# Moving the stage buffers to the bottom of SBUF and everything that lives throughout above them

## The reference

```python
def swiglu_ffn(h, w_gu, w_down):
    gate, up = jnp.split(h @ w_gu, 2, axis=-1)       # 1024 -> 2 x 2816
    return (jax.nn.silu(gate) * up) @ w_down         # 2816 -> 1024

for i in range(2):
    x = x + 0.5 * swiglu_ffn(rms_norm(x, norm_g[i, 0]), ffn_w_gu[i, 0], ffn_w_down[i, 0])
    h = rms_norm(x, norm_g[i, 1])
    x = x + (gla_mixer(h, ...) if i == 0 else diff_mixer(h, ...))
    x = x + 0.5 * swiglu_ffn(rms_norm(x, norm_g[i, 2]), ffn_w_gu[i, 1], ffn_w_down[i, 1])
...
x = x + gate * (concat([y_lru, y_att]) @ w_out)      # the hybrid layer
```

## Time and profile before

| | us |
|---|---|
| median of three runs | 2256.18 |
| the profiled execution, whole | 2258.16 |
| its span, first to last instruction | 2256.3 |
| TensorE (PE) busy | 2230.7 |
| VectorE (DVE) busy | 1260.9 |
| ScalarE (ACT) busy | 918.7 |
| GpSimd (POOL) busy | 155.6 |

### The profile page before, as it was taken

How to read it: one execution, slowest core, us unless ns; L and a number is a source line. 1 busy time by engine, 2 the same in 40 slices (tenths; PEclk the granted TensorE clock), 3 DMA queues, 4 the chain that set the end, 5 groups by cost and what they waited for, 6 DMA issues and landing times.

```text
span 2256.3 us, 24793 instructions
## 1 busy us (share of the span) xinstructions
PE 2230.7 (99%) x9880; PEld 1788.9 (79%) x9880; DVE 1260.9 (56%) x1958; ACT 918.7 (41%) x1446; POOL 155.6 (7%) x128
## 2 busy tenths in 40 slices
PE   9999999999999999999999999999999999999999
PEld 7888888877688888888888887777678888877777
DVE  6443445978654434454434446777566535555863
ACT  4322233567433223333322235777443223237672
POOL 3000003000030000030000021000120000020000
PEclk9999999999999999999999999999999999999999
DMA  6223224121135242242223223222134434232221
GB/s 207 87 84 112 98 70 133 38 94 57 43 101 177 66 133 82 70 136 93 76 94 112 84 84 110 73 73 91 56 122 152 137 112 131 89 131 70 63 73 38
DMA packets 201763, 217.40 MB, mean 96 GB/s; under 512 B 4984, under 2 KB 194552, under 8 KB 201648
## 3 DMA queue, kind: packets, MB, share of 16 engines
q1 hardware_dynamic: 194960, 193.48, 26.4%
q0 software_dynamic: 6544, 22.26, 2.9%
q10 hardware_dynamic: 144, 0.08, 0.0%
HBM read 213.66 MB, written 6.32 MB: 97 GB/s over the span
## 4 chain that ended last, share of the span: by engine, by line
PE 94%; DVE 3%; ACT 2%; issue 1%; DMA 0%; SPq 0%; DVEq 0%; ACTq 0%
PE ps L1606 92%; PE ps L1610 1%; ACT sb_xh L638 1%; DVE sb_xl L1095 0%; ACT sb_whi L638 0%; DMA sb_xT<-xT 0%; DVE sb_wlo L1090 0%; ACT sb_hyb_th L638 0%; ACT sb_lnb L638 0%; DVE sb_hyb_rq L1496 0%; DVE sb_hyb_q L1510 0%; ACT sb_hyb_pt L638 0%; ACT sb_hyb_k L638 0%; ACT sb_dif_k L638 0%; DVE sb_dif_p L1383 0%
## 5 line engine op out<-in xcount | busy, mean ns | idle before, releaser
L1606 PE MATMUL ps<-sb_xh,sb_whi 128*128 128x512 f32 x2120 | 844.9, 399 | 12.8 <-DVE sb_xl L1397 4.9
L1606 PE MATMUL ps<-sb_xl,sb_whi 128*128 128x512 f32 x2120 | 828.6, 391 | 0.1
L1606 PE MATMUL ps<-sb_xh,sb_wlo 128*128 128x512 f32 x2120 | 824.1, 391 | 0.0
L1090 DVE TENSOR_TENSOR sb_wlo<-sb_raw,sb_whi 128x1024 fp32r<-128x1024 f32 (+2 forms) x401 | 473.7, 1185 | 484.3 <-ACT sb_whi L638 483.1
L638 ACT ACTIVATE sb_whi<-sb_raw 128x1024 fp32r<-128x1024 f32 (+2 forms) x401 | 386.9, 968 | 568.5 <-PE ps L1606 561.5
L1606 PEld LDWEIGHTS ps<-sb_xh,sb_whi 128*128 128x128 f32 x2120 | 399.5, 188 | 105.3 <-issue 17.3
L1606 PEld LDWEIGHTS ps<-sb_xl,sb_whi 128*128 128x128 f32 x2120 | 399.8, 189 | 87.3 <-issue 4.6
L1606 PEld LDWEIGHTS ps<-sb_xh,sb_wlo 128*128 128x128 f32 x2120 | 399.3, 188 | 85.3
L1606 PE MATMUL ps<-sb_ffn_ah,sb_whi 128*128 128x512 f32 x704 | 277.6, 394 | 0.0
L1606 PE MATMUL ps<-sb_ffn_ah,sb_wlo 128*128 128x512 f32 x704 | 276.0, 392 | 0.0
L1606 PE MATMUL ps<-sb_ffn_al,sb_whi 128*128 128x512 f32 x704 | 273.3, 388 | 0.0
(11 more groups left out here) (259 smaller groups left out, 1769.2 us busy)
## 6 DMA issues: line engine op xcount, KB each, us to landing
sb_raw<-ffn_w_gu SPq DMA_DIRECT2D x86, 1024.0 KB, 5.2
sb_raw<-ffn_w_down SPq DMA_DIRECT2D x32, 1024.0 KB, 4.9
sb_raw<-gla_w_in SPq DMA_DIRECT2D x12, 1024.0 KB, 5.3
sb_raw<-diff_w_in SPq DMA_DIRECT2D x12, 1024.0 KB, 5.2
sb_ada_raw<-w_ada POOLq DMA_DIRECT2D x12, 1024.0 KB, 6.3
sb_raw<-w_in SPq DMA_DIRECT2D x10, 1024.0 KB, 5.3
sb_raw<-ffn_w_down SPq DMA_DIRECT2D x16, 512.0 KB, 3.6
sb_raw<-ffn_w_down SPq DMA_DIRECT2D x16, 256.0 KB, 2.7
```

The lines of the kernel that those rows point to most:

```text
L1090: e.tensor_tensor(lo, raw[panel % NRAW][:, 0:nk, off:off + 128], hi.bitcast(F32), ALU.subtract).then_inc(sem["w_lo"], 1)
L1606: return e.matmul(out, lhsT, rhs, start=start, stop=stop, skip_group_check=skip)
```

## The change

The list of tensors that stay open is moved below the stages' blocks in the code, and behind a placeholder `stages` of 21,792 float32 (87,168 bytes) per partition that covers the same bytes as the largest stage. The stages' common base becomes 16,512. Within the list the order changes as well: `xh`, `xl`, `xT`, the small tensors, the weight slots, and `raw` at the top. Two lists that name `sqs` and `sq` are completed after these are opened. The instructions of the built program and their order on each engine are the same; only addresses differ.

```diff
+STAGE = 21792
...
-        raw = [sb(f"raw{i}", [128, KT, 256]) for i in range(NRAW)]
-        whi = [sb(f"whi{i}", [128, KT, 128], F32R) for i in range(NSLOT)]
-        wlo = [sb(f"wlo{i}", [128, KT, 128], F32R) for i in range(NSLOT)]
-        x = sb("xT", [128, KT, S])
-        xh = sb("xh", [128, KT, S], F32R)
-        xl = sb("xl", [128, KT, S], F32R)
-        par = sb("par", [128, NCOLS])
...
-            hpb = [t_(f"p{i}", [128, S]) for i in range(2)] + [sqs]
+            hpb = [t_(f"p{i}", [128, S]) for i in range(2)]
...
+        sb("stages", [128, STAGE])
+        xh = sb("xh", [128, KT, S], F32R)
+        xl = sb("xl", [128, KT, S], F32R)
+        x = sb("xT", [128, KT, S])
+        par = sb("par", [128, NCOLS])
+        cst = sb("cst", [128, 3, 128])
+        rb = sb("rb", [128, S])
...
+        whi = [sb(f"whi{i}", [128, KT, 128], F32R) for i in range(NSLOT)]
+        wlo = [sb(f"wlo{i}", [128, KT, 128], F32R) for i in range(NSLOT)]
+        raw = [sb(f"raw{i}", [128, KT, 256]) for i in range(NRAW)]
+        hpb.append(sqs)
```

More of the change, by code:

```diff
@@ L478, in build @@
             lw = HPT[:, 0:2, :].rearrange("p j (t c) -> p j t c", c=128)
-            lru_ln = [HPT[:, 2, :], HPT[:, 3, :], sq[:, :], HPT[:, 0, :]]
             hst = [t_(f"st{i}", [128, 8]) for i in range(3)]
+        sb("stages", [128, STAGE])
[5 more added lines that the diff above has]
+        rb = sb("rb", [128, S])
+        lnb = sb("lnb", [128, S])
+        sqs = sb("sqs", [128, S])
+        sq = sb("sq", [128, S])
+        small = sb("small", [128, 96])
+        ada = sb("ada", [128, 24])
+        lam, neg_b, rbcol = small[:, 56:64], small[:, 64:72], small[:, 72:76]
+        ones, ident, blk = cst[:, 0, :], cst[:, 1, :], cst[:, 2, :]
+        bias_vec = nc.dram_tensor("bias_vec", (8, 1024), F32).ap()
+        bias_rep = nc.dram_tensor("bias_rep", (8, 128 * 1024), F32).ap()
+        whi = [sb(f"whi{i}", [128, KT, 128], F32R) for i in range(NSLOT)]
+        wlo = [sb(f"wlo{i}", [128, KT, 128], F32R) for i in range(NSLOT)]
+        raw = [sb(f"raw{i}", [128, KT, 256]) for i in range(NRAW)]
+        hpb.append(sqs)
+        lru_ln = [HPT[:, 2, :], HPT[:, 3, :], sq[:, :], HPT[:, 0, :]]
         first_squares = rb[:, :], lnb[:, :], ffn_mem[0][3][1][:, :]
```

## The result

The changed kernel takes 2291.47 us (median of 4, 2289.76 to 2294.18) against 2256.27 us before (2255.85 to 2256.99): a ratio of 1.0157, 95% interval 1.0139 to 1.0174. It is slower by 35 us where I forecast 6 us faster, and far outside the range. The profiled execution took 2292.99 us, its span 2291.2 us, 34.9 us more than before.

What follows compares the result with a forecast made beforehand. TensorE bounds the kernel; 5.6 + 0.5 + 0.3 = 6.4 us gained, less a little for reappearing waits, 6.2 us, takes the median from 2256.18 to 2250.0 us. Forecast's own range 2248.3 to 2251.7, overall 2247.5 to 2263.

Steps and rivals of the forecast that it cites:

- What bounds the kernel: Whole kernel: TensorE is busy 2230.7 of 2256.3 us; only the time per matmul and 25.6 us of waits can move.
- Stage tiles as moving operands: Down projections and hybrid's output projection: 2304 matmuls each lose a 2.6 ns price for beginning at 64 modulo 128; 5.6 us gained.
- the passages: Switches between x and stage tiles, eight each way: their extra time goes if all tiles cost the same; 0.5 us gained.
- Weights at 64 modulo 128: Weight slots' new remainder under all 8664 matmuls: taken to cost nothing, from the interval 1397.86 to 1398.09, 230 against 226.6 ns.
- The upper bound: Most the weights' new remainder could cost: the moving operand's 2.6 ns for each of 8664 matmuls, 22.5 us.
- only the offset between moving tile and weights counts: Case inside a slower rival (2272.5 us, chance 0.09): offset 64 in the slow stretches before, 64 in all after.
- the weights' place: Rival, slower: weights' new address costs what the moving operand's does, 16.3 us more, 2272.5 us; chance 0.09.
- 64 everywhere: Claim within a slower rival: after the change, every moving tile lies at offset 64 from its weights.
- The border at byte 131,072: Rival, slower: tiles above that byte are slow, so upper `xl` tiles become slow; 2252.1 to 2267.5 us; chance 0.14.
- No part: Rival, no change: addresses don't matter, down projections are slower by something that goes with the stage; 2256.2 us; chance 0.10.
- Scores: Mixers' `dif_k`, `dif_kl` matmuls (0.4 us) with linear attention's plain float32 matmuls and transposes (0.2 us): half counted, 0.3 us gained.
- VectorE, DMA: Weights' split and panel loads at new addresses: hidden under 10.9 us of TensorE per panel, cost nothing; mixers' waits +-0.5 us.

## Why the prediction was wrong

*What bounds the kernel.* Right: the chain is PE's, and the 34.9 us of the span match the 35.1 us by which the records of the x matmuls grew. The observation on which I built was right too: 226.6 ns in one kind of stretch and 229.2 in the other, the same in every window, is an effect of addresses and not of contention: 192 bytes of padding took it away.

*Stage tiles as moving operands.* This step failed. I gave the 2.6 ns to the moving tile's own remainder modulo 128. The stages' tiles got remainder 0 and kept 229 ns; with everything moved by 64 bytes it stayed so. What held was the distance to the weights: 64 before, 64 modulo 256 after. With 192 bytes of padding it becomes 0, and then the gain that I worked out for this step (5.6 us, and 0.5 for the passages) is there: 2250.5 us against the forecast 2250.0. The size was right, and the cause wrong; that the gain came to the forecast's number in that layout says nothing for the remainder.

*Weights at 64 modulo 128.* This is the failed step that made the loss: a term that I took as nothing and that measured 35 us. I took nothing, on one interval of the earlier trace rows in which `dif_q` is loaded while `xh` streams; the distance is 192 there, and matmuls alone, with all weights at that distance, take 233.4 ns. The row reads 230 at two decimals and I called it no cost. One interval can't show it. In the trace it is 226 ns, and the four of the scores behind it are 228, 230, 233 and 231: what the switch cost came after the interval that I read. In the same way, single intervals of a steady down projection are 232, 226 and 229 ns in turn, and only their mean, 229, is the price. The upper bound was wrong as well. It took the 2.6 ns of distance 64 for the worst that an address can do, and the other distances cost 6 to 8 ns. At 7 ns, 8664 matmuls are 61 us and not 22.5. The loss of 6360 x 5.5 ns = 35 us lies between, since only the x tiles came to such a distance. What the runs showed in the place of this step: not where the weights lie, but that they no longer lie at distance 0 from x. That distance went to 192 modulo 256, at which an x matmul takes 233.5 ns instead of 226.6.

*The rivals.* I named the mechanism, "only the offset between moving tile and weights counts", with 0.09 in one rival with the weights' place, and wrote "64 everywhere" after the change. That was read modulo 128. Modulo 256 the two were 192 and 64, and I had both tables of addresses. The price followed from the wrong modulus. "64 everywhere" would have made x as slow as the stages, 229 ns; it became 233.5. The border at byte 131,072 is excluded twice: the stages' tiles, now below it, stayed slow, and with all at 0 the upper tiles of `xl` and the weights lie above it and are fast. "No part" is excluded by the 192 bytes, with which every tile still begins on a 16-byte line. By the Trainium skill (TensorE: Matmul & The Clock Gate, on what happens when you issue a matmul) the two read ports keep a weight load from slowing the stream; here the distance alone makes 226.6 or 234.3 ns with nothing else running, so the measurement decides, at least for float32r.

*Scores, passages, VectorE, DMA.* The scores of `dif_k` with `dif_q` kept their time (455 and 456 ns); both operands moved together, so their distance stayed, and the 0.3 us that I took for them had the same wrong cause. The passages lost their extra price, as I had taken it, though x and the stages still differ in their distance: in the changed kernel the first twelve intervals after a switch to stage tiles take 2.75 us, which is 12 x 229 ns, and those after the way back 2.79, no more than 12 x 233.5; in the kernel before they were 2.76 and 2.77, of which 2.72 would be 12 x 226.6. That is half a microsecond beside the 35. That the weights' split and the DMA stay hidden was right.

*What remains open.* What in TensorE is slowed, and which operands' distance it is. Neither the distance to a matmul's own weights, nor that to the weights loaded meanwhile, nor each change of remainder explains all settings. In the steady settings short and long intervals follow in a fixed order (232, 226, 229 ns at distance 64), which suggests that something carries over from one matmul to the next; what, no run here shows. Shown are the period of 256 bytes, that 0 is the fast distance at 512 columns, and that the same distance costs the same, within 1 ns, in every layout tried.

## What to carry to other kernels

Before trusting a layout, list for each hot matmul the start of the moving tile minus the start of the weights, modulo 256. In float32r with 512 columns keep it at 0; a change that "only moves buffers" can cost 1.6%, and 192 bytes of padding can give 0.25%. At 256 columns 0 was not the fast distance, so other shapes need their own measurement. When a trace shows two levels of one operation, write down every relation of its addresses, own remainders and differences, at several moduli, before naming one the cause; and do not bound an unknown by the one price that happens to be visible.

## What was not expected of the hardware

A float32r matmul of 512 columns with its own LDWEIGHTS takes 226.6 ns from start to start at best and 228.9 to 234.3 ns at other distances; a start 4 bytes off is already out of the fast place (232.6 ns). The same in bfloat16 takes 216 ns at any distance tried. That is the gap which the Trainium skill (TensorE: Matmul & The Clock Gate, on the back-to-back issue gap) gives for single matmuls, 512 / 2.4 + 2.5 ns, about 216. For a stream in which each matmul has its own LDWEIGHTS the same section gives some 131 ns; the stream here is of that kind and took 216, so there the measurement decides. In float32r even the best is 11 ns above it. At 256 columns the order turns round (120.0 ns at distance 0, 117.8 at 192).
